# Moving one projection into an expert loop, and regrouping the small matmuls around it, in a hybrid decoder step

## The reference

```python
def trunk(x, p, ...):
    hn = rmsnorm(h, g_mix)
    z = hn @ w_in                      # u | q | k | v | o | i~ | f~ | gate_ssm | gate_mlstm
    ys = s5_mixer(u, ...)
    ym = mlstm_mixer(q, k, v, ig, fg, o, ...)
    merged = sigmoid(gs) * (ys @ w_ssm_up) + sigmoid(gm) * (ym @ w_ml_up)
    h = h + merged @ w_out
    h = h + moe_ffn(rmsnorm(h, g_ffn), ...)
    gate = sigmoid(rmsnorm(h, g_ple) @ w_ple_gate)
    h = h + gate * (p @ w_ple_proj)    # the "PLE projection": p has 256 columns
    return rmsnorm(h, g_final)

def s5_mixer(u, ...):                  # 32 groups of 16 channels, 64 complex states each
    bu_r, bu_i = einsum('blgh,gph->blgp', ug, bbar_r), einsum(..., bbar_i)
    xr, xi = associative_scan(...)     # x_t = abar * x_(t-1) + bu_t, complex
    y = einsum('blgp,ghp->blgh', xr, c_re) - einsum('blgp,ghp->blgh', xi, c_im) + d_skip * ug
    y = gelu(y)
    return y * sigmoid(y @ w_glu + b_glu)

def moe_ffn(x, ...):                   # 32 experts, top 4 of each token, softmax weights
    g = x[tok] @ w_gate[e] + b_gate[e]
    u = x[tok] @ w_up[e] + b_up[e]
    g, u = minimum(g, 7), clip(u, -7, 7)
    row = (g * sigmoid(1.702 * g) * (u + 1)) @ w_down[e] + b_down[e]
```

## Time and profile before

| what | value |
|---|---|
| median of three runs | 1376.95 us (1374.84 to 1377.3) |
| the profiled execution | 1376.01 us, its span 1374.2 us |
| PE busy | 1327.2 us, 97% of the span |
| DVE, ACT, POOL busy | 431.1, 263.4, 36.5 us |
| DMA | 448.32 MB, 326 GB/s over the span |
| L1600, gate, up and down matmuls | 677.5 us of PE |
| norm, z tiles, S5 | 0 to 200 us, PE busy 182.33 |
| mLSTM, up-projections, w_out | about 200 to 342 us |
| router, projection, first gather | about 342 to 366 us |
| expert loop | 366 to 1318 us |
| PLE gate, final norm, stores | 1318 to 1374.2 us, PE busy 41.22 |

### The profile page before, as it was taken

How to read it: one execution, slowest core, us unless ns; L and a number is a source line. 1 busy time by engine, 2 the same in 40 slices (tenths; PEclk the granted TensorE clock), 3 DMA queues, 4 the chain that set the end, 5 groups by cost and what they waited for, 6 DMA issues and landing times.

```text
span 1374.2 us, 14828 instructions
## 1 busy us (share of the span) xinstructions
PE 1327.2 (97%) x5767; PEld 588.4 (43%) x5767; DVE 431.1 (31%) x697; ACT 263.4 (19%) x456; POOL 36.5 (3%) x54
## 2 busy tenths in 40 slices
PE   6999899999999999999999999999999999999986
PEld 5666577755433333333333333333333333333332
DVE  4589744432322221213212122221212212121223
ACT  2666340101201111010111101111010111101123
POOL 3000110010000000000000000000000000000000
PEclk9999999999899999999999999999999999999999
DMA  9333154084499999999999999999999999999911
GB/s 289 109 92 92 62 157 153 16 311 157 152 372 422 422 422 421 422 422 422 422 423 422 422 422 421 423 422 422 422 421 423 422 422 422 422 423 422 422 77 39
DMA packets 90457, 448.32 MB, mean 326 GB/s; under 512 B 9148, under 2 KB 36384, under 8 KB 40768
## 3 DMA queue, kind: packets, MB, share of 16 engines
q1 hardware_dynamic: 89616, 446.83, 80.8%
q0 software_dynamic: 816, 1.15, 0.4%
HBM read 444.12 MB, written 3.84 MB: 326 GB/s over the span
## 4 chain that ended last, share of the span: by engine, by line
PE 90%; DVE 5%; ACT 3%; issue 1%; DMA 0%; ACTq 0%; DVEq 0%; SPq 0%
PE bank L1600 48%; PE bank L1270 8%; PE bank L1612 7%; PE bank L1561 6%; PE bank L1594 4%; PE bank L1670 3%; PE bank L1499 3%; PE bank L1383 2%; ACT hnT L715 1%; PE bank L1623 1%; PE bank L1542 1%; PE bank L1304 1%; PE bank L1403 1%; PE bank L1574 1%; PE bank L1248 1%
## 5 line engine op out<-in xcount | busy, mean ns | idle before, releaser
L1600 PE MATMUL bank<-ring,hnT 128*64 128x512 f32 x3072 | 677.5, 593 | 9.0 <-ACT hnT L715 9.0
L1600 PEld LDWEIGHTS bank<-ring,hnT 128*64 128x64 f32 x3072 | 226.1, 137 | 427.1 <-issue 427.1
L1270 PE MATMUL bank<-hnT,ring 128*128 128x320 f32 x576 | 166.8, 442 | 1.2 <-DVE hnT L782 1.2
L1164 DVE TENSOR_SCALAR zT<-bank 128x512 f32<-128x512 f32 x32 | 22.1, 692 | 446.9 <-PE bank L1600 446.9
L1270 PEld LDWEIGHTS bank<-hnT,ring 128*128 128x128 f32 x576 | 107.1, 192 | 44.8 <-issue 5.4
L1612 PE MATMUL bank<-att,zT 128*128 128x512 f32 (+1 forms) x204 | 97.8, 614 | 1.3 <-ACT att L720 1.3
L1166 DVE TENSOR_SCALAR zT<-bank 128x512 f32<-128x512 f32 x32 | 22.1, 692 | 225.1 <-PE bank L1600 225.1
L1561 PE MATMUL bank<-xkv,zT 128*64 128x512 f32 x396 | 90.8, 592 | 0.0
L1179 DVE TENSOR_TENSOR zT<-zT,bank 128x512 f32<-128x512 f32 (+1 forms) x102 | 69.9, 685 | 51.5 <-PE bank L1612 51.5
L720 ACT ACTIVATE att<-bank 64x512 f32<-64x512 f32 x64 | 37.8, 591 | 233.0 <-PE bank L1600 232.3
L688 ACT ACTIVATE hnT<-bank 128x512 f32<-128x512 f32 x33 | 19.7, 597 | 288.4 <-PE bank L1561 288.4
(11 more groups left out here) (365 smaller groups left out, 873.8 us busy)
## 6 DMA issues: line engine op xcount, KB each, us to landing
ring<-in_w_gate SPq DMA_DIRECT2D x128, 1024.0 KB, 16.4
ring<-in_w_up SPq DMA_DIRECT2D x128, 1024.0 KB, 18.7
ring<-in_w_down SPq DMA_DIRECT2D x128, 1024.0 KB, 14.5
ring<-in_w_in SPq DMA_DIRECT2D x18, 1024.0 KB, 5.6
ring<-in_w_out SPq DMA_DIRECT2D x4, 1024.0 KB, 9.7
ring<-in_w_ple_gate SPq DMA_DIRECT2D x4, 1024.0 KB, 19.8
ring<-in_w_ssm_up SPq DMA_DIRECT2D x2, 1024.0 KB, 5.5
ring<-in_state_ml_c SPq DMA_DIRECT2D x4, 512.0 KB, 6.7
```

Of the source, the lines that this page charges most:

```text
L1164: V.tensor_scalar(mg, bank[0][:, :], LIMIT, None, ALU.min).then_inc(g_ready, 1)
L1270: last = mm_(bank[z_bank(n)][:, 0:NT], wz[:, k, half * P:half * P + P], hn3[:, k, :], start=k == 0, stop=k == KD - 1)
L1600: last = mm_(dst[64 * hf:64 * hf + 64, :], srcT[:, (k % 4) * P + 64 * (k // 4):(k % 4) * P + 64 * (k // 4) + 64], w3(s, 2, D)[:, k % 2, 51 ...
```

## The change

**S5 stage.** `masked_u` and its tile go. `bu(j, part)` computes one part (0 real, 1 imaginary) by four matmuls, each on one 32-row strip of z tile j and of the weights, into four banks (`BU_BANK`); z tiles take three banks instead of four. Part 0 of the next step stands ahead of the last z tile of the step, part 1 behind it, and ACT copies in the same order. `turns(0)` and `sines(0)` stand ahead of the z copies on ACT, `reduce_turns(0)` ahead of the coefficient work's rest on DVE. `y(j - 1)` stands behind two z tiles of its step instead of ahead of them.

**Router.** Logits of tile 2 go to a bank of their own, and DVE adds the router's bias and takes the top 8 tile by tile. The PLE projection leaves this place.

**Experts.** The loop is split at MID = 8 turns on PE and ACT, and the whole projection stands between the halves, with three banks (`PJ_BANK`). w_ple_proj gets a place of its own (`wpj`), loaded by SP behind expert 0's w_down once POOL's nine stores are done; slot 11 takes w_down at once. Both bias tables stand in one tile of 64 rows, and a constant `hot` selects row e of both; the two biases of an expert are one step of four matmuls (two row strips by two column halves), ahead of `gate_up`. The third token tile of `acc` is folded during the loop: its right 512 columns stand on partitions 64 to 127 (one ACT copy ahead, one behind), and `scatter` and `accumulate` have five steps, the last of two column halves.

**Behind the experts.** Tiles 0 and 1 are transposed from `acc` itself; their root goes into the scale of the sigmoid. The value loads on PE and DVE stand ahead of the last scatter and accumulate. Tile 2 is finished and stored in two halves; ACT's squares of tiles 0 and 1 stand together, and a square root of a constant (`table_in`) stands ahead of tile 2's squares.

The diff, cut to its core:

```diff
-        USED0 = [5, 4, 4, 4, 3, 3, 0, 0, 1, 1, 1, 2]
+        USED0 = [5, 4, 4, 4, 3, 3, 0, 0, 1, 1, 1, 1]
...
-        PJ_BANK = [0, 1, 3, 7]
+        PJ_BANK = [6, 7, 3]
+        MID = NR // 2
+        BU_BANK = [3, 4, 5, 6]
 
         def z_bank(n):
-            return n % 4 if n < ZGM else 0
+            return n % 3 if n < ZGM else 0
...
             sp.dma_start(wr_sb.rearrange("p (t i e) -> p t i e", t=4, i=2), t["w_router"][0].rearrange("(t p i) e -> p t i e", p=P, i=2)).then_inc(wr_full, 16)
             sp.wait_ge(out_done, 5)
-            load(11, rows256("w_ple_proj", 0))
             for s in range(8, RING):
-                if s == 11:
-                    sp.wait_ge(pj_done, 6)
                 load_first(s)
+            sp.wait_ge(stored_pool, 16 * 9)
+            sp.dma_start(wpj, rows256("w_ple_proj", 0)).then_inc(ple_full, 16)
...
-            def masked_u(j):
+            def bu_evac(j, part):
+                if j:
+                    act.wait_ge(rotin_done, j)
                 for i in range(NI):
-                    a(um[:, i * NT:i * NT + NT], Z(ZU + j), ACT.Copy, scale=c("imask")[:, i:i + 1]).then_inc(um_ready, 1)
+                    q = NI * part + i
+                    act.wait_ge(bu_done, 8 * j + q + 1)
+                    a((bu_r, bu_i)[part][:, i * NT:(i + 1) * NT], bank[BU_BANK[i]][:, 0:NT], ACT.Copy).then_inc(bu_ready, 1)
...
-            masked_u(0)
             act.wait_ge(xT_done, 2 * TT)
             turns(0)
+            sines(0)
+            for n in range(4):
+                z_evac(n)
+
+            for n in range(4):
+                act.wait_ge(bxT_done, n + 1)
+                dst = (BT, CT)[n // 2][:, n % 2]
+                a(dst.rearrange("p j q -> p (j q)"), bank[4 + n][:, :], ACT.Copy).then_inc(bct_ready, 1)
+            z_evac(4)
+            act.wait_ge(stT_done, 1)
+            a(h0T, bank[7][:, 0:256], ACT.Copy).then_inc(stT_ready, 1)
+            a(n0T[:, 0:32], bank[7][:, 256:288], ACT.Copy).then_inc(stT_ready, 1)
+            bu_evac(0, 0)
             z_evac(5)
             for j in range(NJ):
-                if j:
-                    act.wait_ge(rotin_done, j)
-                for q in range(8):
-                    act.wait_ge(bu_done, 8 * j + q + 1)
-                    dst = (bu_r, bu_i)[q % 2][:, (q // 2) * NT:(q // 2 + 1) * NT]
-                    a(dst, bank[4 + q % 3][:, 0:NT], ACT.Copy).then_inc(bu_ready, 1)
-                if j == 0:
-                    sines(0)
-
+                bu_evac(j, 1)
...
+            with act.Fori(0, MID) as p:
+                pair_act(p)
+            for k in range(2):
+                act.wait_ge(pTt_done, k + 1)
+                a(pT[:, k, :], bank[k][:, 0:NT], ACT.Copy).then_inc(pT_ready, 1)
+            for n in range(6):
+                w = TW[n // 2]
+                act.wait_ge(pj_done, n + 1)
+                a(pproj[n // 2][0:w, (n % 2) * 512:(n % 2) * 512 + 512], bank[PJ_BANK[n % 3]][0:w, :], ACT.Copy).then_inc(pj_ready, 1)
+            with act.Fori(MID, NR) as p:
+                pair_act(p)
...
-                link(V.tensor_tensor(lg[0:w, tt, :], bank[6][0:w, 32 * tt:32 * tt + 32], brb[0:w, :], ALU.add))
-            for tt in range(TT):
+                dve.wait_ge(rl_done, max(tt + 1, 2))
+                link(V.tensor_tensor(lg[0:w, tt, :], bank[6 + tt // 2][0:w, 32 * tt:32 * tt + 32], brb[0:w, :], ALU.add))
                 link(V.max(mtop[:, tt, :], lg[:, tt, :]))
...
-                for m in range(6):
+                for m in range(5):
                     tt, hf = m // 2, m % 2
-                    w = TW[tt]
-                    dve.wait_ge(sc_done, n * 6 + m + 1)
-                    A = acc[0:w, tt, 512 * hf:512 * hf + 512]
-                    V.tensor_tensor(A, A, bank[6 + m % 2][0:w, :], ALU.add).then_inc(acc_add, 1)
+                    dve.wait_ge(sc_done, n * 5 + m + 1)
+                    A = acc[:, tt, 512 * hf:512 * hf + 512]
+                    V.tensor_tensor(A, A, bank[6 + m % 2][:, :], ALU.add).then_inc(acc_add, 1)
...
             z_tile(4)
             pe.wait_ge(bct_ready, 4)
             pe.wait_ge(st_full, 48)
-            tr(bank[4][:, 0:P], h0_rows_r, ident)
-            tr(bank[4][:, P:2 * P], h0_rows_i, ident)
-            tr(bank[4][:, 256:288], n_rows[0:32, :], ident[0:32, 0:32]).then_inc(stT_done, 1)
-            z_tile(5)
-            pe.wait_ge(stT_ready, 2)
-
-            def bu(j):
-                for q in range(8):
-                    m = 8 * j + q
-                    if q % 2 == 0:
-                        pe.wait_ge(um_ready, 4 * j + q // 2 + 1)
-                    if m >= 3:
-
-                        pe.wait_ge(bu_ready, 8 * j + q - 2 if q >= 3 else 8 * j)
-                    mm_(bank[4 + q % 3][:, 0:NT], BT[:, q % 2, j, :], um[:, (q // 2) * NT:(q // 2 + 1) * NT],
+            tr(bank[7][:, 0:P], h0_rows_r, ident)
+            tr(bank[7][:, P:2 * P], h0_rows_i, ident)
+            tr(bank[7][:, 256:288], n_rows[0:32, :], ident[0:32, 0:32]).then_inc(stT_done, 1)
+
+            def bu(j, part):
+                if j or part:
+                    pe.wait_ge(bu_ready, 8 * j + NI * part)
+                for i in range(NI):
+                    r = slice(32 * i, 32 * i + 32)
+                    mm_(bank[BU_BANK[i]][:, 0:NT], BT[r, part, j, :], Z(ZU + j)[r, :],
                         start=True, stop=True).then_inc(bu_done, 1)
...
+            logits(2)
+            def ple_proj():
+                pe.wait_ge(ple_full, 32)
...
+                pe.wait_ge(ple_full, 48)
+                pe.wait_ge(acc_add, 2 + 5 * MID)
+                pe.wait_ge(pT_ready, 2)
+                for n in range(6):
+                    tt, hf = n // 2, n % 2
                     w = TW[tt]
+                    if n >= 3:
+                        pe.wait_ge(pj_ready, n - 2)
+                    for k in range(2):
+                        last = mm_(bank[PJ_BANK[n % 3]][0:w, :], pT[:, k, tt * P:tt * P + w], wpj[:, k, 512 * hf:512 * hf + 512], start=k == 0, stop=k == 1)
+                    last.then_inc(pj_done, 1)
+                pe.wait_ge(pj_ready, 6)
...
-                for m in range(6):
+                for m in range(4):
                     tt, hf = m // 2, m % 2
-                    w = TW[tt]
-                    pe.wait_ge(acc_add, n * 6 + (m + 1))
-                    mm_(bank[6 + m % 2][0:w, :], p_all[:, tt * P:tt * P + w], yb[:, 512 * hf:512 * hf + 512], start=True, stop=True).then_inc(sc_done, 1)
+                    pe.wait_ge(acc_add, n * 5 + max(m + 1, 2))
+                    mm_(bank[6 + m % 2][:, :], p_all[:, tt * P:tt * P + P], yb[:, 512 * hf:512 * hf + 512], start=True, stop=True).then_inc(sc_done, 1)
+                pe.wait_ge(acc_add, n * 5 + 5)
+                for hf in range(2):
+                    last = mm_(bank[6][64 * hf:64 * hf + 64, :], p_all[:, 2 * P:2 * P + 64], yb[:, 512 * hf:512 * hf + 512], start=True, stop=True)
+                last.then_inc(sc_done, 1)
 
             def gate_up(n, picked):
                 pe.wait_ge(xsT_ready, picked)
                 pe.wait_ge(oh_ready, picked)
-                project(n, 0, xsT, bank[0], g_done, bias=0)
-                project(n, 4, xsT, bank[1], u_done, bias=1)
+                for b in range(2):
+                    r = slice(NE * b, NE * b + NE)
+                    for hf in range(2):
+                        mm_(bank[b][64 * hf:64 * hf + 64, :], onehot[r, :], btab[r, 512 * hf:512 * hf + 512], start=True, stop=False)
+                project(n, 0, xsT, bank[0], g_done, True)
+                project(n, 4, xsT, bank[1], u_done, True)
...
+            with pe.Fori(0, MID) as p:
+                pair(p)
+            ple_proj()
+            with pe.Fori(MID, NR) as p:
+                pair(p)
             pe.wait_ge(cnt_ready, 1)
             extra = pe.value_load(cnt_i[0:1, 0:1], min_val=0, max_val=EXTRA)
+            scatter(NR, 4 * NR + 1)
...
-            transposes(2, 0)
-            transposes(2, 1)
+            transposes(2, 0, extra)
+            transposes(2, 1, extra)
             ple_gate(0)
-            transposes(2, 2)
+            transposes(2, 2, extra)
             ple_gate(1)
             ple_gate(2)
```

274 lines of the change are left out of this document (134 added, 140 removed).

## The result

The changed kernel takes 1344.83 us (median of four, 1344.51 to 1345.96) where the kernel before takes 1376.6: ratio 0.9773, with a 95% interval of 0.9756 to 0.979. 1342 was forecast, the range was 1334 to 1356. The profiled execution took 1344.88 us, its span is 1343.1.

A forecast was written before the change was run, and what follows sets the result against it. DMA was taken to bound the expert loop at 59.64 us a pair, with PE nearly as full. 1376.0 - 15.3 (S5) - 4.7 (ahead of experts) - 5.5 (loop) - 8.1 (tail) = 1342.4, say 1342; range 1334 to 1356.

The forecast's parts named there:

- What bounds the loop: Expert loop: DMA needs 59.64 us a pair whatever PE does, so the loop gains only 5.5 us.
- the spare 4.7: End of expert loop: the last w_up load lands 4.7 us before PE reads it, time the loop can gain.
- the pause: PLE projection between pairs 8 and 9: 13.3 us on PE that cost nothing, since freed slots' loads cover it.
- S5 strips: S5 stage: four row strips side by side and a new order start the GLU at 173.8, -15.3 us.
- the part: S5 stage: one bu part of four row-strip matmuls takes 0.55 us, all four at once.
- strips in sequence: Rival: row strips don't overlap; S5 gains 9 us, the loop 0.4, time 1354; chance 0.14.
- Ahead of the experts: Router to first bias: projection leaves PE and ACT, ranks start at once; -4.7 us (-4.7 to -7.1).
- The half clock that I did put into the sum: Ahead of the experts: ranks at half clock end 3.5 us after their start, not 2.1; gather comes out 1 to 2 late.
- The tail: Behind the experts: shorter gap, scatter and first gate tile; -8.1 us (-5 to -9).
- The gap: Scatter's end to gate's first matmul: 7.5 us falls to 2.5 (addition 0.7, branch 0.4, two evacuations of 0.69), -5.0.
- More than 422 GB/s: Rival: DMA can give more than 422 GB/s, so the loop follows PE, -27.7 us, time 1320; chance 0.07.
- PE's clock falling in the loop: Rival: PE's clock falls while it waits for slots, making the kernel slower, 1411 at a share of 0.10; chance 0.05.

The follow-up runs named there:

- fewer bytes: Changed kernel, but the last w_gate and last w_up load of each of experts 1 to 31 bring half their bytes: 1333.05 us.
- the second trace: The changed kernel itself, unaltered, measured and profiled again beside two later variants: 1343.49 us (1342.06 to 1346.4).
- the run: Changed kernel, but all four matmuls of a bu part use row strip 0, so they can't run side by side: 1354.97 us.
- PE kept busy: Changed kernel plus five unread 128x320 matmuls on PE behind the last logits: 1341.88 us.

## Why the prediction was right, and where it was off

**What bounds the loop**: right, and the step on which the sum turned. That DMA needs 59.64 us a pair was read from landing times alone; pairs that wait take 59.63 and 59.69. The gain of 5.5, the spare 4.7 plus 0.8, measured 5.60; in four other traces with the same loop it is 5.2 to 6.6 (940.00 to 941.38 us). How it splits into the two terms isn't shown. PE waits from the sixth pair on, and again from the sixth behind the pause, where I had some four pairs. PE's own pair is 57.1, not 56.5. Half of that is the four-part step, 1.02 us (345.58 to 346.60) and not 0.86; the other half is 0.15 us per expert in the steps on either side of it (a `down` takes 7.02 us up to the bias, 369.39 to 376.41, where it took 6.92 before). By the same reasoning this is hidden, and the experiment with fewer bytes shows it. That the pause is nearly free between the pairs, and why, held in two experiments: 13.4 ahead of the loop, 10.5 ahead of the last pair, 1.0 at MID.

**S5 strips**: the mechanism right, the size off by 1.5 in this trace and 0.8 in the second. The term mis-sized was the part: 0.75 us instead of 0.55, with 0.15 more in the z tile behind it (4.51 from 74.93 to 79.44; the five ahead of the part take 4.35 each). DVE's waits were 3.85 and 1.84 where 3.2 and 2.4 were worked out. A term left out is `y(3)`: it starts at 169.43, because its bank is read by DVE's last operation (168.74 and 0.55 long) first, which I had not put on the path. That DVE started at 49.63 instead of 48.8 can't be put on either: in nine other traces with this S5 code it starts between 47.97 and 49.42, and the GLU between 173.71 and 176.84, around the forecast 173.8. The sentence that DVE's first rotation comes early was right and worth nothing by itself. For strips in sequence I had -9; the run has -6.0.

**Ahead of the experts**: 6.70 instead of 4.7, inside its bounds, and by luck of the execution. From the GLU's start to the mask it took 161.06 before and takes 158.04: 3.0 less where I had 1.1. Before, PE had been at half clock already ahead of the ranks (granted 0.50 from 341 to 345 us), so logits and transposes cost more than their instructions; in this execution they ran at full clock up to the last logits. In eight other traces with this code the last logits took 1.86 to 1.92 us, as before the change (1.91), and not 1.12; there the GLU and the first bias are 171.86 to 173.51 us apart, a gain of 3.4 to 5.0. The half clock that I did put into the sum came: ranks 4.05 us, gather 4.43.

**The tail**: -4.96 instead of -8.1, the step that failed. Of its terms the scatter measured 0.85 as forecast, the gate's first tile 1.60 instead of 2.2, the span's end 0.44 instead of 0. The gap was the miss: 2.5 us were left in the sum for addition, branch and evacuations, and 5.43 are left. I had 0.4 for a branch where PE stands for 2.41, and forgot the sixteen transposes that still stand between scatter and gate: 3.02 us here, partly at half clock behind the stand, about 2.2 where there is no stand. Addition and evacuations, which I did count, hide. Without the stand the forecast would nearly have come out, for the wrong reason: in the two traces in which PE doesn't stand the same tail gains 8.6 us (52.86 and 52.89 instead of 61.50). What PE stands for isn't shown; the packets above point to the loading of its code.

**The rivals.** Row strips in sequence: excluded, 0.82 against 2.42 a part. More than 422 GB/s: excluded, the rate is 421 to 422 in every stretch of the loop from 450 us on. The Trainium skill, DMA: Bandwidth & Descriptors, Specifications, has a ceiling of 435 GB/s; no run here came to it in the loop. PE's clock falling in the loop: excluded for the changed kernel, 1.00 in every stretch; waits of 0.55 us a slot did not lower it.

The errors had different signs: 1.5 and 3.1 too much, 2.0 too little. The total is better than its parts, and that is luck. In the second trace, where the clock ahead of the experts was nearer to the forecast's, the stages moved by -14.50, -4.97, -5.20 and -4.93: the tail is the one error of size.

## What to carry over

When two engines are full at once, let the landing times say which is slower: a time from issue to landing that grows steadily is a queue that falls behind, and its growth per turn is the difference of the two rates. What the faster engine saves there is worth only the spare that is left at the end; what it has to spare is one sum, which a block of other work can use up if enough turns lie behind it. Of a gap that an edit shortens, list the instructions that stay in it, one by one, before the difference is taken. And when leaving code out takes a stand away, look at traces that keep the code: here two of them had no stand either.

## Not expected of the hardware

Four row strips of 32 rows run 3.1 times as fast as four matmuls on one strip (0.75 against 2.35 us), and the z tile between two such parts takes 4.51 us instead of 4.35. Behind the last scatter PE stands for 2.41 us, with nothing in the trace to wait for, in front of code that a branch doesn't run; it doesn't stand without that code, and it doesn't in two kernels that keep it and have more matmuls elsewhere. In each of the seven traces with the stand a packet of instructions moves at its start. Ahead of the scatter, with the branch there, PE stood for 1.49 in one kernel and 3.09 in another, the 1.30 us for ACT's copies among them. And executions of one kernel differ by up to 10 us (PE kept busy: 1334.97 to 1344.86). The traces show a part of such a spread: the same ranks took 4.05 us at half clock and about 2.1 at full clock, and the GLU of the same S5 code started between 173.71 and 176.84. Where the fastest executions won the rest is in no trace.
